# Down products of two SwiGLU stages from seven half products, with hidden tiles in groups of 8, 8 and 6

## What is computed

```python
def swiglu(x, wg, wu, wd):
    hid = silu(x @ wg) * (x @ wu)          # 1024 -> 2816
    return hid @ wd                        # 2816 -> 1024

x = layer_norm(ALPHA * x + 0.5 * swiglu(x, ffn1_wg, ffn1_wu, ffn1_wd), ln1_g, ln1_b)
z = x @ w_in                               # gated short convolution and pooling branch, merged to m
x = layer_norm(ALPHA * x + m @ w_out, ln2_g, ln2_b)
x = layer_norm(ALPHA * x + 0.5 * swiglu(x, ffn2_wg, ffn2_wu, ffn2_wd), ln3_g, ln3_b)
```

## Time and profile before

| | |
|---|---|
| Median of 3 runs | 1088.27 us (1088.27 to 1089.12) |
| The profiled execution | 1087.43 us, its span 1085.6 us |
| PE busy | 1054.4 us, 97% |
| DVE busy | 688.7 us, 63% |
| POOL busy | 525.6 us, 48% |
| ACT busy | 437.2 us, 40% |
| Mean granted TensorE clock | 0.993 |

### The profile page before, as it was taken

How to read it: one execution, slowest core, us unless ns; L and a number is a source line. 1 busy time by engine, 2 the same in 40 slices (tenths; PEclk the granted TensorE clock), 3 DMA queues, 4 the chain that set the end, 5 groups by cost and what they waited for, 6 DMA issues and landing times.

```text
span 1085.6 us, 20864 instructions
## 1 busy us (share of the span) xinstructions
PE 1054.4 (97%) x8731; PEld 1047.7 (97%) x8731; DVE 688.7 (63%) x1019; ACT 437.2 (40%) x658; POOL 525.6 (48%) x311
## 2 busy tenths in 40 slices
PE   8899999999999988999999999989999999999996
PEld 7899999999999988999999999988999999999996
DVE  6999921288846865342625427989996016886486
ACT  4565532155553443222231324445555113555234
POOL 4355654154568246444453546324565433566321
PEclk9999999999999999999999999999999999999999
DMA  8134234233355042242342335103334323433402
GB/s 256 36 102 117 77 100 117 78 100 116 98 137 136 15 108 75 68 117 72 90 117 67 114 93 144 40 2 97 114 94 125 88 69 98 117 99 88 121 26 79
DMA packets 195002, 103.30 MB, mean 95 GB/s; under 512 B 4420, under 2 KB 193428, under 8 KB 194901
## 3 DMA queue, kind: packets, MB, share of 16 engines
q1 hardware_dynamic: 194827, 101.85, 33.0%
q10 hardware_dynamic: 82, 0.12, 0.1%
HBM read 99.74 MB, written 2.48 MB: 94 GB/s over the span
## 4 chain that ended last, share of the span: by engine, by line
PE 85%; DVE 10%; issue 2%; ACT 2%; DMA 1%; POOL 0%; SPq 0%; ACTq 0%; DVEq 0%; POOLq 0%
PE ps L1303 14%; PE ps L1323 14%; PE ps L1320 14%; PE ps L1321 14%; PE ps L1305 14%; PE ps L1304 14%; DVE x L1179 1%; DVE xl L925 1%; DVE x L1160 1%; DVE form_lo L976 1%; DMA raw<-in_ffn_wd_dram 1%; DMA xrow<-in_x_prompt_dram 1%; PE ps L1426 1%; PE ps L1366 1%; PE ps L1416 0%
## 5 line engine op out<-in xcount | busy, mean ns | idle before, releaser
L569 POOL TENSOR_TENSOR wl<-raw,wh 128x512 fp32r<-128x512 f32 x120 | 221.6, 1874 | 226.2 <-DVE raw L951 182.3
L615 ACT ACTIVATE wh<-raw 128x1024 fp32r<-128x1024 f32 (+3 forms) x203 | 238.4, 1178 | 191.9 <-DMA raw<-in_ffn_wd_dram 102.2
L1303 PE MATMUL ps<-form_hi,wh 128*128 128x260 f32 x640 | 182.3, 285 | 5.1 <-ACT temps L615 5.1
L1305 PE MATMUL ps<-form_hi,wl 128*128 128x260 f32 x640 | 181.6, 284 | 0.0
L1304 PE MATMUL ps<-form_lo,wh 128*128 128x260 f32 x640 | 181.6, 284 | 0.0
L1320 PE MATMUL ps<-xh,wh 128*128 128x260 f32 x640 | 167.9, 283 | 3.8 <-DVE ymix L1253 3.8
L1321 PE MATMUL ps<-xl,wh 128*128 128x260 f32 x640 | 167.3, 283 | 0.0
L561 POOL TENSOR_TENSOR wl<-raw,wh 128x1536 fp32r<-128x1536 f32 (+2 forms) x36 | 108.1, 3010 | 107.1 <-ACT wh L615 107.1
L1320 PE MATMUL ps<-hid_hi,wh 128*128 128x260 f32 x544 | 141.9, 282 | 0.0
L1321 PE MATMUL ps<-hid_lo,wh 128*128 128x260 f32 x544 | 141.8, 283 | 0.0
L1303 PE MATMUL ps<-xh,wh 128*128 128x260 f32 x480 | 136.8, 285 | 2.1 <-DVE temps L983 1.5
(11 more groups left out here) (225 smaller groups left out, 2354.7 us busy)
## 6 DMA issues: line engine op xcount, KB each, us to landing
raw<-in_ffn_wg_dram SPq DMA_DIRECT2D x80, 256.0 KB, 3.3
raw<-in_w_in_dram SPq DMA_DIRECT2D x40, 512.0 KB, 3.9
raw<-in_ffn_wd_dram SPq DMA_DIRECT2D x16, 768.0 KB, 5.7
b<-in_ffn_wu_dram SPq DMA_DIRECT2D x40, 256.0 KB, 3.4
raw<-in_ffn_wu_dram SPq DMA_DIRECT2D x40, 256.0 KB, 3.0
raw<-in_ffn_wd_dram SPq DMA_DIRECT2D x16, 640.0 KB, 5.4
raw<-in_w_out_dram SPq DMA_DIRECT2D x7, 512.0 KB, 3.9
xrow<-in_x_prompt_dram SPq DMA_DIRECT2D x4, 512.0 KB, 5.3
```

What stands on the lines that cost most here:

```text
L569: nc.gpsimd.tensor_tensor(wl_slot[:, s, :], raw_slot[:, s, :], wh_slot[:, s, :].bitcast(F32), ALU.subtract).then_inc(lo_ready, 1)
L615: return nc.scalar.activation(out, in_, ACT.Copy)
L1303: mm(out, hi, vh, start=start and n == 1, stop=False, skip_group_check=more)
L1305: ins = mm(out, lo, vh, start=False, stop=n == count, skip_group_check=more)
```

## The change

Down products of the first 16 hidden tiles are made as the pairs are, from seven half products. A list `UNITS` puts 20 "up" units and 8 "down" units in one row: up 2 to 8, four down units of group 0 (hidden tiles 0 to 7), up 9 to 16, four down units of group 1 (tiles 8 to 15), up 17 to 21. A down unit makes two output tiles, from the even and the odd hidden tiles of its group, and has 84 matmuls for 8 hidden tiles. Only the last 6 hidden tiles stay plain (`down_tiles`, then `closing`).

The sums of activations for a down unit are new work: three for each two hidden tiles (`mid_sums`, `mid32`), one more (`fourth_sum`, put into the free quarter of `xh` and `xl`), their rounding on ACT (`round_mid`) and remainders on DVE (`mid_rest`). The results of a down unit are added to x32 from `first_p`, `first_u`, `first_q` and three banks in six DVE instructions instead of two `part`. Sigmoid and a DVE product become Silu on ACT (L1012, L1016 and L983 go). ACT's order inside a unit changes: the sums T1 and T3 are rounded first, then the gate, then the three loaded blocks. Down loads of 6 blocks are split by POOL in two instructions.

```diff
-    SPANS = ((2, 12), (12, KF))
-    HELD = (12, KF - 12)
+    GROUPS = (8, 8, 6)
+    UNITS = [None]
+    for g in range(len(GROUPS)):
+        for f in range(max(GROUP_AT[g], 2), GROUP_AT[g] + GROUPS[g]):
+            UNITS.append(("up", f))
+            if g and f == GROUP_AT[g]:
+                UNITS += [("down", g - 1, j) for j in range(K // 2)]
...
+            def round_mid(f):
+                act.wait_ge(s.mid_made, MID_NO[f])
...
+                    first = step.on(tt(mid32[:, 0, i, :], even32[:, 1, :], bank(pair, 1), ALU.subtract))
+                    if i == 0:
+                        fourth_sum(i)
+                    dve.wait_ge(s.mid_step, first)
+                    second = step.on(tt(mid32[:, 1, i, :], mid32[:, 0, i, :], even32[:, 0, :], ALU.subtract))
+                    dve.wait_ge(s.mid_step, second)
+                    tt(mid32[:, 2, i, :], mid32[:, 1, i, :], bank(pair, 0), ALU.add).then_inc(s.mid_made, 1)
...
+                def down_first(p):
...
+                    tt(a, a, first_p, ALU.add).then_inc(p_taken, 1)
+                    tt(b, b, first_uq, ALU.add).then_inc(u_taken, 1)
...
+                    stt(a, bank(q, 0), 0.5, a, ALU.mult, ALU.add)
...
+                    stt(b, bank(2, q), 0.5, b, ALU.mult, ALU.add).then_inc(s.part, 1)
...
-                        pe.wait_ge(s.up1, f - 3)
-                    half_product("Q5", "T1", f, z_bank)
+                        pe.wait_ge(u_taken, no - 2)
+                    if down:
+                        pe.wait_ge(s.mid_ready, MIDS[UNITS[p][1]])
+                    half_product("Q5", "T1", p, z_bank)
...
+                def fourth(p):
+                    pe.wait_ge(t24_ready, unit_no(n, p))
+                    pe.wait_ge(q_taken, unit_no(n, p))
```

840 lines of the change are left out of this document (480 added, 360 removed).

## The result

The changed kernel takes 1132.6 us (median of 4 runs) against 1088.3: 1.041 times the time of before, with a 95% interval of 1.039 to 1.042. The prediction was 1107 us, slower, with a range that ended at 1123. The direction is right, and the size is not.

What follows compares the result with a forecast made beforehand. PE bounds the kernel, with DVE level in scaled pairs and 1.4 us in reserve in unscaled ones. Sum: 1087.4 - 23.0 - 5 + 12 + 35 = 1106.4, plus 0.9 for the median: 1107 us, range 1070 to 1123.

Steps and rivals of the forecast that it cites:

- Bound of the kernel, and the sign: Pairs: PE and DVE level where the residual is scaled, DVE 1.4 us in reserve otherwise; slower overall, chance 0.65.
- Matmuls, -23.0: Down products: 96 fewer matmuls in each of two stages at 0.120 us, -23.0 us if PE is the bound everywhere.
- Opening, -5: Start of each stage: shorter DVE chain and smaller gaps save 2.5 us a stage, -5 us, between -2 and -7.
- Closing, +12: First finished output tile to last addition: DVE becomes the bound, giving back 5.0 + 7.2 us, between +3 and +20.
- DVE's term, +35: Up and down units: DVE's new work and waits for POOL add 17.5 us a stage, bounds +12 and +52.
- the walk: Two up units, POOL and DVE taking turns: 21.1 us unscaled, 1.6 more with scalings; 6 and 3 us per stage's runs.
- The rival at 1132 us: Worse port: three full waits in each unit, +52, and the closing given back in full, +20; chance 0.10.
- Signs: Units: DVE above 95% busy to the 24th, `up_second` period 10.4 to 11.4 us; closing: PE idle 5 to 7 us.

Runs made afterwards that it cites:

- e2: Changed kernel with POOL's three remainders of each unit's blocks cut from 512 to 8 columns: 1092.1 us.
- e10: Changed kernel with new chunk slots, later sum remainders, residual scaling on ScalarE, transposes in TensorE's end wait, and POOL's unit remainders cut to 8 columns: 1080.0 us.
- e4: Kernel before the change, with only Silu in place of Sigmoid and DVE's multiplication: 1086.9 us, 0.999 of before.
- e6: e1 with ScalarE rounding the last two down chunks ahead of its squares of tiles 1 to 3 in the closing stretches: 1120.1 us.
- e1: Changed kernel with only the slot table of the mix chunks altered, so late mix and output chunks take the longest-free slot: 1118.5 us.
- e8: e1 with 30 transposes of the identity in TensorE's wait at the end, before the first transposes of rows: 1114.0 us.

## Why the prediction was right in direction and wrong in size

- *Bound of the kernel, and the sign.* Right. The scaled pairs had no room on DVE and the unscaled ones 1.4 us, and what the change puts on DVE showed as gaps of TensorE at the named places: before Q4, before P1 after an odd tile, before the first down unit's Q5. That the gaps come from POOL's and DVE's turns is shown by e2: it takes 14.0 us from a stage's units.
- *Matmuls, -23.0.* Right as a count (8539 against 8731). As a gain it is not there in any run. It is a net of +5.8 us in the units and -17.3 us in the closing stretch of each stage, and the stretch gives back a part of its share whatever is done to the units (e10).
- *Opening, -5.* Wrong. It was nothing in stage 1 (46.99 to 47.48) and 1.3 us in all in e4. The step took DVE's saved time as the chain's; behind the multiplication a wait for ScalarE's copy takes over, which the row already names as the releaser.
- *Closing, +12.* Right in size: 8.3 + 4.7 = 13.0, by stretches that are 9.0 and 12.6 shorter where 17.3 went (10.1 and 12.3 forecast). The way there was not as told. DVE was to be the bound with almost no idle time; it idles 3.3 and 4.2 us, TensorE's waits for POOL's down chunks are a part of the length (e6), and what bounds the rest is not shown. The first stage's forecast was also made on a window that is too long, 50.1 us up to 380.34, where the last addition is at 377.09.
- *DVE's term, +35.* Right in size, in part by luck: from the first P6 to the first closing tile stage 1 is 24.1 us longer, of which 5.8 are the 48 matmuls that moved ahead of this point, so 18.3; stage 2 by the same reckoning 17.6 (with its gain in the opening in it). Forecast 17.5 a stage. In detail, unscaled pairs 20.92 (forecast 21.1), scaled 22.0 (22.7), down units 10.24 to 10.58 (10.6 to 11). All three are a little lower, so that from the first `up_second` on a stage loses 14.3 us (296.4 against 276.3, less 5.8). What the walk missed is the start of a stage, some 4 us: Q4 of the first unit waits 2.4 to 2.6 us, and the clock is low behind it. DVE has the new sums of tile 1 there beside everything that it does for the first units; that these are the cause is not tested. The two errors nearly cancel. The sum of the walk has a slip besides: three pairs at +1 and +1.6 are 7.8, not 6.
- *Not in the sum at all: the failed step.* The moved slots: 14.1 us by e1, and by the table at most 12.9 (9.0 and 3.9). `MIX_AT` and `OUT_AT` stand in the diff, and the prediction costs them at nothing without a word, since the mix itself was not changed. Of the 25 us missed it is about half. What the runs showed in its place is a late load: a rounding on ScalarE that stands 11.2 us for it, and TensorE 8.04 us behind that. The missing clock term is the second: at the end, 3.7 us by the table and 3.5 by e8's tail. I had TensorE idle in the last closing stretch, but looked only at its length and not at what comes after it. Between the spans the forecast was 19.0 us and 43.8 came; of the 24.8 missed, the slots are up to 12.9, the end 3.7, the opening 5.0, the closing 1.0, DVE's term 0.9 and the two small rows of the table 1.4.
- *The rival at 1132 us.* Its time was nearly the result, its reason was not: DVE's term was not 26 a stage, and the closing was not given back in full.
- *Signs.* DVE was to be over 95% busy up to unit 24; it is at 94% (67.86 of 72) in the scaled stretch and at 91% (52.73 of 58) in the other. The rest of its time it waits for ScalarE's roundings and for TensorE, and TensorE for it, so that neither is full in the units. In the units the period of `up_second` alternates (11.82 and 9.10), 10.46 on average, where each was to be 10.4 to 11.4; after unit 24 the periods are 10.39 and 9.80, 10.1 on average, as forecast. TensorE idles 4.8 and 4.1 us in the closing stretches, not 5 to 7. What stays open is how much of the gap of 2.75 us in stage 1's closing is POOL's queue and how much its turns with DVE (e6 only excludes ScalarE's order), and where e8 got its last microsecond.

## What to carry to other kernels

Count what a change saves where it is saved: here the matmuls went from a stretch in which DVE was nearly as busy as TensorE, and came partly back in one in which DVE had no room at all. Read every table that the diff touches, those of buffer slots first, even in a stage whose arithmetic is the same, and ask for each load which product frees its slot and who stands in order behind the rounding that waits for it. Where GpSimd and DVE both work on SBUF, keep GpSimd's instructions short (512 columns beat 1536 here by 30 us; shorter ones were not tried), and keep DVE's two-input instructions that TensorE waits for away from them.

## What the runs showed of the hardware

- The length of one GpSimd instruction alone, with the same work, was worth 30 us: three of 512 columns 1118.5, one of 1536 columns 1148.5. A DVE instruction of 260 columns then took 3.58 us. I had expected 12 us at most.
- A DVE instruction with one input in SBUF meets GpSimd as well: the scaling (one tensor in, a constant) shows up to 1.53 us and 1288 ns on average in the changed kernel, and 0.42 to 0.43 us in the units of e2, where GpSimd is quiet.
- After a wait of 4.1 us TensorE ran at 0.50 for 17.1 us from 1094.6 on in e1, although it had transposes and small products to do for most of the first ten; with 3.44 us of transposes in that wait (e8) it stayed at 1.00 through the same work.
- A DVE instruction's duration holds its wait: cut to 8 columns, the one on L1118 that stands where GpSimd works still shows 679 ns, its sister on L1116 151 ns.
